# A decoder layer in float32: another order of the seven products in each feed-forward step, later residual adds, and the second block of x ahead of the first weights

## The reference, cut to what matters

```python
D_MODEL, SEQ, D_FF = 2048, 256, 5632          # one sequence of 256 tokens, float32
x = x + 0.5 * swiglu(rmsnorm(x, ffn1_norm), gate, up, down)
h = rmsnorm(x, mix_norm)                      # then two token mixers (dilated and forgetting
...                                           # attention), sigmoid-gated and projected
x = x + merged @ w_out
x = x + 0.5 * swiglu(rmsnorm(x, ffn2_norm), gate, up, down)
return rmsnorm(x, final_norm)

def swiglu(x, w_gate, w_up, w_down):
    return (silu(x @ w_gate) * (x @ w_up)) @ w_down
```

## Time and profile before

| | us |
|---|---|
| median of 3 runs (lowest, highest) | 2120.27 (2119.47, 2120.48) |
| profiled execution, its time | 2120.27 |
| its span in the trace | 2118.5 |
| busy: TensorE matmuls and transposes | 2085.8 |
| busy: VectorE | 1612.2 |
| busy: ScalarE | 1095.8 |
| busy: GpSimd | 2.6 |

### The profile page before, as it was taken

How to read it: one execution, slowest core, us unless ns; L and a number is a source line. 1 busy time by engine, 2 the same in 40 slices (tenths; PEclk the granted TensorE clock), 3 DMA queues, 4 the chain that set the end, 5 groups by cost and what they waited for, 6 DMA issues and landing times.

```text
span 2118.5 us, 26539 instructions
## 1 busy us (share of the span) xinstructions
PE 2085.8 (98%) x9475; PEld 1729.6 (82%) x9475; DVE 1612.2 (76%) x1613; ACT 1095.8 (52%) x1259; POOL 2.6 (0%) x7
## 2 busy tenths in 40 slices
PE   7999999999999999999999999999999999999997
PEld 5888888888888788888888888878888888888886
DVE  6899888899888744444455655688998888998886
ACT  5555555555555444554454344465555555555553
POOL 0000000000000000000000000000000000000000
PEclk9999999999999999999999999999999999999999
DMA  7656566656566455545445665555565656565652
GB/s 249 212 165 217 179 218 202 206 165 218 179 219 211 145 174 183 181 158 178 153 166 191 198 205 187 191 180 199 177 209 187 218 198 200 176 210 186 218 201 97
DMA packets 202451, 402.88 MB, mean 190 GB/s; under 512 B 6416, under 2 KB 6592, under 8 KB 202272
## 3 DMA queue, kind: packets, MB, share of 16 engines
q1 hardware_dynamic: 202032, 401.64, 56.7%
q0 software_dynamic: 160, 0.46, 0.1%
q10 hardware_dynamic: 208, 0.08, 0.0%
HBM read 400.06 MB, written 2.10 MB: 190 GB/s over the span
## 4 chain that ended last, share of the span: by engine, by line
PE 95%; DVE 2%; ACT 1%; issue 1%; DMA 0%; ACTq 0%; SPq 0%; DVEq 0%
PE ps L521 21%; PE ps L523 21%; PE ps L522 21%; PE ps L536 6%; PE ps L534 6%; PE ps L535 6%; PE ps L698 3%; PE ps L699 3%; PE ps L700 3%; PE ps L586 1%; DVE w_lo L1187 1%; ACT w_hi L912 0%; DVE xres L1295 0%; ACT chunk_buf L949 0%; ACT xT_hi L937 0%
## 5 line engine op out<-in xcount | busy, mean ns | idle before, releaser
L1187 DVE TENSOR_TENSOR w_lo<-raw,w_hi 128x1024 fp32r<-128x1024 f32 x256 | 312.7, 1225 | 306.9 <-ACT w_hi L912 306.5
L912 ACT ACTIVATE w_hi<-raw 128x1024 fp32r<-128x1024 f32 x256 | 269.9, 1058 | 309.1 <-PE ps L523 309.0
L925 ACT ACTIVATE w_hi<-raw 128x1024 fp32r<-128x1024 f32 x280 | 297.1, 1061 | 224.0 <-PE ps L700 99.4
L1221 DVE TENSOR_TENSOR w_lo<-raw,w_hi 128x1024 fp32r<-128x1024 f32 x280 | 342.4, 1223 | 80.6 <-ACT w_hi L925 67.4
L521 PE MATMUL ps<-w_hi,xT_hi 128*128 128x512 f32 x816 | 322.2, 395 | 7.9 <-DVE w_lo L1187 7.4
L523 PE MATMUL ps<-w_hi,xT_lo 128*128 128x512 f32 x816 | 319.1, 391 | 0.0
L522 PE MATMUL ps<-w_lo,xT_hi 128*128 128x512 f32 x816 | 318.9, 391 | 0.0
L1221 DVE TENSOR_TENSOR more_lo<-raw,more_hi 128x1024 fp32r<-128x1024 f32 x160 | 195.9, 1224 | 44.3 <-ACT more_hi L925 34.8
L925 ACT ACTIVATE more_hi<-raw 128x1024 fp32r<-128x1024 f32 x160 | 169.8, 1061 | 114.0 <-PE ps L523 89.8
L521 PE MATMUL ps<-w_hi,hT_hi 128*128 128x512 f32 x576 | 224.3, 389 | 0.0
L523 PE MATMUL ps<-w_hi,hT_lo 128*128 128x512 f32 x576 | 224.1, 389 | 0.0
(11 more groups left out here) (215 smaller groups left out, 3587.7 us busy)
## 6 DMA issues: line engine op xcount, KB each, us to landing
raw<-in_ffn_w_gate SPq DMA_DIRECT2D x88, 1024.0 KB, 5.2
raw<-in_ffn_w_up SPq DMA_DIRECT2D x88, 1024.0 KB, 5.1
raw<-in_ffn_w_down SPq DMA_DIRECT2D x88, 1024.0 KB, 5.0
raw<-in_w_in SPq DMA_DIRECT2D x80, 1024.0 KB, 5.0
raw<-in_w_out SPq DMA_DIRECT2D x16, 1024.0 KB, 5.0
raw<-in_w_proj_dil SPq DMA_DIRECT2D x8, 1024.0 KB, 5.0
raw<-in_w_proj_fox SPq DMA_DIRECT2D x8, 1024.0 KB, 4.9
xres<-in_x SPq DMA_DIRECT2D x4, 512.0 KB, 7.1
```

The source lines that it names most:

```text
L912: nc.scalar.activation(slot_hi(place, offset), raw_half(place, offset), ACT.Copy).then_inc(hi_ready, 1)
L925: nc.scalar.activation(slot_hi(place, offset), src, ACT.Copy).then_inc(hi_ready, 1)
L1187: nc.vector.tensor_tensor(slot_lo(place, offset), raw_half(place, offset), slot_hi(place, offset).bitcast(F32), ALU.subtract).then_inc(lo_ ...
L1221: nc.vector.tensor_tensor(slot_lo(place, offset), step_source(r)[0], slot_hi(place, offset).bitcast(F32), ALU.subtract).then_inc(lo_ready, 1)
```

## The change

1. The seven products of a paired group stand in another order: T3, T1, gate (odd rows), T4, gate (even rows), T2, up, where they stood T3, up, T1, T2, T4, gate, gate. Their banks go with them, so that slab 2 now writes bank 4 (GATE) and slab 6 bank 7 (UP0).
2. T3 and T1 are made together and earlier (`early_sums`), ahead of the splits of slab 10 and of the last slab (29) of a step; T2 and T4 behind the splits of a group's slabs 0 and 1.
3. The loads of gate and up come in the order gate, up in every group; the loads 4 and 8 wait for later splits (5 and 16 in place of 2 and 13).
4. TensorE waits once, ahead of slab 2, for all residual adds of the step before and for the whole hidden tile; before, it waited ahead of slab 1 (three adds) and slab 4 (all). At the end of a step it waits for three adds in place of two.
5. On VectorE the residual adds stand behind the split of their turn in place of ahead of it; the hidden tile is made in turn 22 in place of 23, and, in a pass's first 16 slabs, at the end of turn 15 in place of its beginning. The parts of the up product are added one turn earlier.
6. Start: block 1 of x goes through transposing, scaling, rounding and splitting ahead of the first slabs. The three small loads are issued by ScalarE, and the forget weights' and tables' copies move from turns 11 and 12 to turn 15.

```diff
-PRODUCTS = (("sum", T3), ("up", 1), ("sum", T1), ("sum", T2), ("sum", T4), ("gate", 1), ("gate", 0))
+PRODUCTS = (("sum", T3), ("sum", T1), ("gate", 1), ("sum", T4), ("gate", 0), ("sum", T2), ("up", 1))
-FREE = (-6, -4, -2, 0, 2, 7, 9, 11, 13, 18, 20, 22)
+FREE = (-6, -4, -2, 0, 5, 7, 9, 11, 16, 18, 20, 22)
...
-    ADDED = {0: 2, "mix": 2 + FF_CHUNKS * NN, 1: 2 + (FF_CHUNKS + NN) * NN}
+    ADDED = {0: 1, "mix": 1 + FF_CHUNKS * NN, 1: 1 + (FF_CHUNKS + NN) * NN}
...
@@ SyncE: load order of a step
-                        order = (up_w, gate_w) if g % 2 else (gate_w, up_w)
-                        for half, w in enumerate(order):
-                            load_step(place, 2 * l + half, w[f][:, CT * g:CT * (g + 1), cols])
+                        load_step(place, 2 * l, gate_w[f][:, CT * g:CT * (g + 1), cols])
+                        load_step(place, 2 * l + 1, up_w[f][:, CT * g:CT * (g + 1), cols])
@@ TensorE: start and step
-                    if b == 0 and o in (0, 1, 3):
+                    if b == 0 and o in (1, 3):
                         transpose_x(0, (o + 3) // 2)
...
-                        (M7, of_pair(S3)), (UP0, of_pair(S4)), (M5, of_pair(S1)), (M6, of_pair(S2)),
-                        (GATE + 1, of_tile(1, 1)), (GATE, of_tile(1, 0)), (M1, of_tile(0, 0)))):
+                        (M7, of_pair(S3)), (M5, of_pair(S1)), (GATE, of_tile(1, 0)),
+                        (GATE + 1, of_tile(1, 1)), (M1, of_tile(0, 0)), (M6, of_pair(S2)),
+                        (UP0, of_pair(S4)))):
...
                     for o in paired(place, 0, 0):
-                        if o == 1:
-
-                            pe.wait_ge(added, base - 1)
                         if o == 2:
                             transpose_tokens(hid, 0, T)
-                        if o == 4:
 
                             pe.wait_ge(hidden_ready, hid + TT)
                             pe.wait_ge(added, base)
...
-                    pe.wait_ge(added, base + 2)
+                    pe.wait_ge(added, base + NN - 1)
...
+            transpose_x(0, 1)
             ffn(0, 0)
@@ ScalarE
-                    if b == 0 and o == FIRST - 5:
+                    if b == 0 and o == 2 * WIDE - 1:
...
             round_x(0, 0)
-            for o in range(2):
+            round_x(0, 1)
+            for o in range(FFN_RING):
                 round_slab(first_place(0), o)
-            round_x(0, 1)
-            for o in range(2, FFN_RING):
-                round_slab(first_place(0), o)
+            act.dma_start(tab[:, P:C_END], table[:, P:C_END]).then_inc(table_landed, 16)
+            act.dma_start(f_raw[:, :, :], in_w[:, :, F_COL:G_COL]).then_inc(forget_landed, 16)
+            act.dma_start(f_bias[:, :], b_forget.broadcast_to([P, HEADS])).then_inc(forget_landed, 16)
@@ VectorE
+            def early_sums(place, q, g):
+
+                gate, up = 0, 1
+                dve.wait_ge(raw_landed[up], place.landed(STEP_LOADS * q + 4 * g + up))
+                nc.vector.tensor_tensor(sums[:, T3], raw[:, up, 1::2, :], raw[:, up, 0::2, :],
+                                        ALU.subtract).then_inc(summed, 1)
+                dve.wait_ge(raw_landed[gate], place.landed(STEP_LOADS * q + 4 * g + gate))
+                nc.vector.tensor_tensor(sums[:, T1], raw[:, up, 0::2, :], raw[:, gate, 0::2, :],
+                                        ALU.subtract).then_inc(summed, 1)
...
-                    if o == FIRST - 1:
-                        dve.wait_ge(slab_done, first.slab(FIRST))
-                        multiply_up([ps[:, FIRST_UP + t] for t in range(TT)], silu)
...
-                    if b == 0 and o == FIRST - 4:
+                    if b == 0 and o == FIRST - 1:
...
+                    if o == FIRST - 1:
+                        dve.wait_ge(slab_done, first.slab(FIRST))
+                        multiply_up([ps[:, FIRST_UP + t] for t in range(TT)], silu)
...
-                        if o > STEP - DOWN and o % 2 == 1:
-                            n = (o - (STEP - DOWN)) // 2
-                            add_down(place, o + 1, n, DOWN_BANKS[n], 0.5)
                         if not last or o + FFN_RING < STEP:
                             split_step(place, o + FFN_RING, i * 8 + count, last)
...
-                        if o == 23:
                             dve.wait_ge(combined, merged + 5)
                             multiply_up([up_sums[:, 1 - t] for t in range(TT)], i * TT + (silu + TT))
+                        if o > STEP - DOWN and o % 2 == 1:
+                            n = (o - (STEP - DOWN)) // 2
+                            add_down(place, o + 1, n, DOWN_BANKS[n], 0.5)
```

More of the change, by code:

```diff
@@ L298, in step_source @@
             return sums[:, which], None
-        l = 4 * g + (what == "gate")
+        l = 4 * g + (what == "up")
         return raw[:, l % LOADS, which::2, :], l
@@ L1195, in sum_of_ups @@
                                         ALU.subtract).then_inc(summed, 1)
+                dve.wait_ge(raw_landed[gate], place.landed(STEP_LOADS * q + 4 * g + gate))
+                nc.vector.tensor_tensor(sums[:, T1], raw[:, up, 0::2, :], raw[:, gate, 0::2, :],
+                                        ALU.subtract).then_inc(summed, 1)
             def split_step(place, offset, count, final=False):
-                gate, up = 1, 0
                 q, r = divmod(offset, STEP)
+                if r in (10, STEP - 1) and not (final and r == STEP - 1):
+                    early_sums(place, *((q, 1) if r == 10 else (q + 1, 0)))
                 kind, g, o = step_slab(r)
-                if r == 10:
-                    sum_of_ups(place, q, 1)
-                if r == 27 and not final:
-                    sum_of_ups(place, q + 1, 0)
-                if kind == "paired":
-                    done = count + 8 * q + 4 * g
-                    if o == 1:
-                        dve.wait_ge(raw_landed[gate], place.landed(STEP_LOADS * q + 4 * g + gate))
-                        nc.vector.tensor_tensor(sums[:, T1], raw[:, up, 0::2, :], raw[:, gate, 0::2, :],
-                                                ALU.subtract).then_inc(summed, 1)
-                    if o == 2:
+                dve.wait_ge(hi_ready, place.slab(offset + 1))
+                nc.vector.tensor_tensor(slot_lo(place, offset), step_source(r)[0],
+                                        slot_hi(place, offset).bitcast(F32), ALU.subtract).then_inc(lo_ready, 1)
+                if kind == "paired" and o in (0, 1):
+                    done, gate = count + 8 * q + 4 * g, 0
+                    if o == 0:
                         dve.wait_ge(summed, done + 1)
@@ L1421, in _ @@
             scale_x(0, 0)
-            for o in range(2):
-                split_slab(first_place(0), o)
             scale_x(0, 1)
-            for o in range(2, FFN_RING):
+            for o in range(FFN_RING):
                 split_slab(first_place(0), o)
```

30 lines of the change are left out of this document (10 added, 20 removed).

## The result

| | median us (lowest to highest, runs) | ratio to before, 95% |
|---|---|---|
| before | 2120.09 (2119.47 to 2120.48, 4) | |
| after | 2142.64 (2140.95 to 2144.67, 4) | 1.0107 (1.0090 to 1.0125) |

The change costs 22.5 us. The prediction was 2132.5, which is 12.5 more than before, with a range up to 2141: the direction was right and the size too small. The profiled execution of after took 2140.0 us (span 2138.2). It is shorter than all four timed runs of its kernel, so the trace explains 19.7 us of span; the other 2.8 us are in no trace.

What follows compares the result with a forecast made beforehand. TensorE was taken as the bound, VectorE close behind. Start -3.7, first steps +3.3, boundaries +12.6 and late load +0.3 gave +12.5 us on 2120.27: 2132.8, rounded to 2132.5; own range 2128 to 2137, 8-in-10 range 2125 to 2141.

Steps and rivals of the forecast that it cites:

- The boundary: Where a step follows a step: slab 2 waits for the later residual add, 0.70 us, 18 times, 12.6 us slower.
- the wait for it at the loop's end comes at 195.88: also met, by less than 0.4 us: End of a step: the third residual add ends at 195.5, before TensorE waits for it, so no stall there.
- The start: Opening of the kernel: with block 1 first, slab 6 starts at 37.8 instead of 41.52, 3.7 us won.
- I cost them at nothing: At the start: three DMA issues moved to ScalarE stand where it waits anyway ahead of slab 6's rounding, so cost nothing.
- the lower bound of 2 us: At the start: least gain, if the DMA issues and their small transfers are felt in ScalarE's chain.
- The first steps: First step of each pass: TensorE waits for the later hidden products, 2.4 us and 0.9 us, together 3.3 us slower.
- the clock: Behind the first step's 2.4 us stop: a fall to half speed would cost about 2 us; only in the upper bound.
- The late load: Ahead of slab 9: load 5, issued later, delays both early sums; 0.3 us in all, as a rival 8 us, 10%.
- The overrun of VectorE: Step's end: VectorE doesn't catch up, its 0.7 us margin eaten; each further 0.7 us costs 12.6 us: 2145, 9%.
- Margin 0.2 us. I take 0.3 us for all 20 steps together: Second token split, seen at 16.4 after slab 0's start, against TensorE's need ahead of slab 9 at 16.6.

Runs made afterwards that it cites:

- both controls: Changed kernel with residual adds ahead of their turn's split again: 2130.16 us; kernel before with only those adds moved behind the split: 2119.56 us.
- all_undone: Changed kernel with small loads back on GpSimd, residual adds ahead of their split, first hidden tile and copies as before: 2121.82 us.
- undone_tokens: all_undone with, in addition, the second token tile rounded and split ahead of turn 5's other work: 2117.21 us.
- before_late_add: Kernel before with one edit, the residual adds behind the split of their turn: 2119.56 us.
- x1_raw_last: Kernel before with block 1 of x ahead of the first slabs and the three small loads on ScalarE, forget weights last: 2116.35 us.

## Why the prediction was right in direction and too small

- **The boundary, 12.6 forecast:** right. The add was to let slab 2 go at 3.80 us after slab 0's undisturbed start; it went at 3.40 + 0.38 = 3.78. 13.1 us in the trace, 12.5 between the medians, with both controls. One detail failed: "the wait for it at the loop's end comes at 195.88: also met, by less than 0.4 us". The third add ended 0.23 us ahead of the place where slab 0 was due, and that was not soon enough: more than half of the stall is paid there, wherever the loop goes round again. The sum didn't suffer, because the fourth add's time is fixed by slab 29 and what is lost at slab 0 isn't lost again at slab 2.
- **The start, -3.7 forecast, -0.15 measured:** the step that failed is "I cost them at nothing", of the three DMA issues. I had looked at what ScalarE waits for otherwise (slab 0, the fourth load) and not at how long an issue can hold its queue; the lower bound of 2 us was also too high. The chain itself was right: with the order turned round slab 6 is at 37.60, against 37.8. This is 3.6 us of the miss.
- **The first steps, 3.3 forecast, 5.5 in the trace, 7.4 between medians:** the stops came out as forecast, 2.5 us for 2.4 in pass 1 and 0.9 for 0.9 in pass 2. What was missing is the clock, which fell behind the first one: 1.6 us. I had the price ("about 2") in the text and left it out of the sum. Since it fell in one profiled execution of six with this stop, leaving it out was no bad bet; after's trace is the unlucky draw.
- **The late load, 0.3 forecast:** the mechanism was right and stood as a rival at 10% with 8 us. In the trace 2.8 us, nearly all of it in the last step of each pass; between medians 4.6 (all_undone to undone_tokens) to 5.9, and 6.6 between those two traces. The step that failed is "Margin 0.2 us. I take 0.3 us for all 20 steps together", which took one landing time, 5.0, for all. Within the loop load 5 landed in 5.1 to 5.5 us and just held behind the boundary's stall; in the last steps it landed in 6.7 and 6.2. This is 2.5 us of the miss, and without the stall the rival's 8 us would have been near.
- **The overrun of VectorE (9%):** it did not happen. The split of slab 5 starts 0.91 us after slab 0 (0.38 us idle before it), so VectorE is free in time, as forecast. Operations of 1.22 us started 1.13 or 1.14 us apart in after too. So the rule of the Trainium skill (VectorE: DVE Perf Modes, "The DRAIN you can't avoid") does not show as a full serialization here; the same section adds that an operation that isn't held starts earlier.

Forecast +12.5; with +3.55 for the start, +2.2 for the first steps, +2.5 for the late load, +0.5 at the boundaries and -1.5 at pass 2's opening it is 19.75, and the span grew by 19.7. So two steps failed, the three DMA issues and load 5's margin, and together they are about 6 of the 7.25 us by which the trace missed the forecast; the two items of the clock, +1.6 and -1.5, happen to cancel in this trace, which is luck. The remaining 2.8 us to the timed median stay open: the clock behind pass 2's opening, which the profiled run was spared, and the load's varying landing are seen to vary by that much between profiles, but the timed runs have no trace.

## What to carry to other kernels

A margin of a few tenths of a microsecond is a cost, not a saving: where a load or an add just makes it in one traced step, price it with the latest landing that any step shows, and look at the steps outside the loop separately. Moving an operation later and its wait earlier are each free and together are not, so read a reordering as pairs of the two. And count a DMA issue with the one ahead of it on its queue: here the load of many small pieces held the issue behind it, and cost nothing as the last. Last, a fall of the clock in one trace can be a draw; look for the same stop in the traces of sibling kernels before it goes into a sum.

## What the runs showed of the hardware that I had not expected

- A DMA issue on ScalarE's queue took 6.77 us behind a load of 2048 pieces of 32 bytes, and the same issue 0.45 us ahead of it. ScalarE's arithmetic behind it waited, 5.73 us.
- The same stop of TensorE (2.53 to 2.55 us, at the opening of pass 2) was followed by the lower level of the clock in nine of the thirteen profiled executions here and by the full clock in four (after, before_late_add, undone_tokens, x1_raw_last). The difference is 1.5 to 1.7 us. A shorter stop (1.88 or 1.89 us, with four transposes behind it) brought the clock to half in one of six. The length of a stop alone doesn't tell.
- A wait at a loop's end that is met only as the last matmul starts costs: 0.61 us to the next matmul instead of 0.23. Where the code goes on outside the loop, a wait met at the same moment gave 0.27. Why wasn't tried.
- Load 5 landed in 4.9 to 5.5 us in the loop's other steps. In the last steps it took 5.0 to 7.5, and in the first step of pass 2 it took 5.1 to 7.3, in the profiles of the changed kernel and its variants. In the six of these profiles that were read for it, a packet or two of the instruction queues moved beside load 5 in these places, and none in four other steps. Whether they delayed the load wasn't tried.
